# A gated delta-rule scan: diagonal inverses for two directions at once, one more unit of look-ahead, and some filler arithmetic on GpSimd

## The reference, cut to what matters

```python
decay = exp(where(tril_incl, g[..., :, None] - g[..., None, :], -inf))
lmat  = where(tril_strict, einsum('bnhid,bnhjd->bnhij', k_beta, k) * decay, 0)
t_inv = triangular_solve(eye + lmat, eye)          # inverse of a unit lower triangle
u, w  = t_inv @ v_beta, t_inv @ (k_beta * exp(g))
a_intra = where(tril_incl, einsum('bnhid,bnhjd->bnhij', q, k) * decay, 0)
def step(state, xs):                                # one chunk after the other
    v_new = u_i - w_i @ state
    o_i = (q_i * exp(g_i)) @ state + a_i @ v_new
    state = state * exp(g_last) + (k_i * exp(g_last - g_i)).T @ v_new
```

## Time and profile before

| | |
|---|---|
| Runs, median (range) | 2976.65 us (2975.73 to 2983.44), 3 runs |
| Profiled execution | 2969.94 us, its span 2968.2 us |
| Mean granted PE clock | 0.945 of full speed |
| Busy, share of the span | PE 91%, VectorE 47%, ScalarE 35%, GpSimd 20% |
| The scan | 553 to 1257 us |

### The profile page before, as it was taken

How to read it: one execution, slowest core, us unless ns; L and a number is a source line. 1 busy time by engine, 2 the same in 40 slices (tenths; PEclk the granted TensorE clock), 3 DMA queues, 4 the chain that set the end, 5 groups by cost and what they waited for, 6 DMA issues and landing times. The chain is left out here.

```text
span 2968.2 us, 46123 instructions
## 1 busy us (share of the span) xinstructions
PE 2691.4 (91%) x18134; PEld 2530.2 (85%) x18134; DVE 1406.6 (47%) x2321; ACT 1040.6 (35%) x1801; POOL 601.8 (20%) x488
## 2 busy tenths in 40 slices
PE   7999999899899999728999868989999999999999
PEld 3898999788788888726777758889999999999999
DVE  4564332156667676447888833352222242222222
ACT  4212333234234343136778733332222222222211
POOL 1001222334333433133223221210111000111100
PEclk9999999989779899858999989999999999999999
DMA  5324664343343332140000044332222233222232
GB/s 202 144 80 131 220 220 158 125 117 95 90 138 86 97 101 72 58 164 14 9 17 16 12 180 167 116 98 71 78 76 72 78 114 94 71 78 71 69 96 70
DMA packets 195643, 294.22 MB, mean 99 GB/s; under 512 B 82800, under 2 KB 121744, under 8 KB 193936
## 3 DMA queue, kind: packets, MB, share of 16 engines
q1 hardware_dynamic: 192592, 276.15, 29.9%
q10 hardware_dynamic: 2880, 15.73, 1.5%
HBM read 228.28 MB, written 63.52 MB: 98 GB/s over the span
## 5 line engine op out<-in xcount | busy, mean ns | idle before, releaser
L277 PE MATMUL f_ps<-mf_h_hi,mf_w_hi 128*128 128x320 f32 x1408 | 435.1, 309 | 1.4 <-PEq L1985 1.4
L277 PE MATMUL f_ps<-mf_h_hi,mf_w_lo 128*128 128x320 f32 x1408 | 435.1, 309 | 0.0
L277 PE MATMUL f_ps<-mf_h_lo,mf_w_hi 128*128 128x320 f32 x1408 | 435.1, 309 | 0.0
L2418 DVE TENSOR_TENSOR mf_w_lo<-mf_w_raw,mf_w_hi 128x1024 fp32r<-128x1024 f32 (+1 forms) x135 | 188.9, 1399 | 431.7 <-ACT mf_w_hi L2270 431.4
L277 PE MATMUL proj_ps<-h_hi,w_hi 128*128 128x320 f32 x896 | 282.9, 316 | 6.0 <-DVE w_lo L571 5.6
L277 PE MATMUL proj_ps<-h_lo,w_hi 128*128 128x320 f32 x896 | 278.2, 311 | 0.0
L277 PE MATMUL proj_ps<-h_hi,w_lo 128*128 128x320 f32 x896 | 278.1, 310 | 0.0
L277 PEld LDWEIGHTS f_ps<-mf_h_hi,mf_w_hi 128*128 128x128 f32 x1408 | 264.4, 188 | 1.6 <-issue 1.6
L277 PEld LDWEIGHTS f_ps<-mf_h_lo,mf_w_hi 128*128 128x128 f32 x1408 | 264.4, 188 | 0.0
L277 PEld LDWEIGHTS f_ps<-mf_h_hi,mf_w_lo 128*128 128x128 f32 x1408 | 264.4, 188 | 0.0
L2344 POOL TENSOR_TENSOR f_ff_lo<-f_ff_f,f_ff_hi 128x640 f32 (+1 forms) x44 | 69.3, 1575 | 783.4 <-ACT f_ff_hi L2270 783.4
(11 more groups left out here) (321 smaller groups left out, 6434.2 us busy)
## 6 DMA issues: line engine op xcount, KB each, us to landing
mf_w_raw<-w_up_dram SPq DMA_DIRECT2D x88, 512.0 KB, 3.5
w_raw<-w_in_dram SPq DMA_DIRECT2D x48, 512.0 KB, 4.3
w_ada_raw<-w_ada_dram SPq DMA_DIRECT2D x16, 1024.0 KB, 5.0
mf_w_raw<-w_mix_dram SPq DMA_DIRECT2D x32, 512.0 KB, 4.8
mf_w_raw<-w_down_dram SPq DMA_DIRECT2D x32, 448.0 KB, 3.3
delta_t<-delta_tile ACTq DMA_DIRECT2D x10, 1024.0 KB, 6.7
decay_t<-g_rows SPq DMA_DIRECT2D x40, 256.0 KB, 4.5
kq_t<-delta_t SPq DMA_DIRECT2D x20, 512.0 KB, 4.5
```

What stands on the lines that cost most here:

```text
L277: ins = nc.tensor.matmul(out, w(k), a(k), start=(first and n == 0 and q == 0), stop=(last and n == len(ks) - 1 and q == 2))
L2418: nc.vector.tensor_tensor(wlo[:, slot, 0:nk], raw[:, slot, 0:nk], whi[:, slot, 0:nk].bitcast(F32), ALU.subtract).then_inc(E[half]["lo"], 1)
```

## The change

- `diagonal` works for the pair of units 2j (forward) and 2j + 1 (backward) at once, on 128 partitions, in `body(u)` of odd u = 2j - 1: rows 1 to 5 in level 4, 6 to 8 in level 5, 9 in level 6, always behind the products. ScalarE turns the backward half's blocks first (`turn_backward`, at the head of odd units) and writes the pair after level 6. SP stores it with four DMAs, later in the odd unit than before (behind slot 8), and loads `x_base` with eight DMAs a unit, each of twice the pieces.
- Products are made three units ahead (`AHEAD`), decay matrices four; the scan opens at unit -4. The products stand behind the first half of levels 5 and 6.
- `kq_t` has two buffers and serves the products alone; the recurrence reads a second copy, `kq_again`, loaded once more. `n_t` and `attn_t` have five buffers. `o_stage` and `fill_stage` have one each.
- `quota` is 6 in all of the units -4 to -1: the same 312 filler matmuls. Filler groups take `bank_F` and an idle bank of `banks_bc` in turn for the first 13 groups.
- From filler tile 8 on the low part is made by GpSimd (`fill` on GpSimd).

```diff
-        H4, NU = 4, 2 * NT
+        H4, NU, AHEAD, RING = 4, 2 * NT, 3, 5
...
-        K_AT = {(LV[1], 1): 0, (LV[2], 1): 1}
+        K_AT = {(LV[1], 0): 0, (LV[2], 0): 1}
-        UNITS = range(-3, NU + 1)
+        UNITS = range(-AHEAD - 1, NU + 1)
...
-        BASE_ROWS = ((1, 2, 3, 4, 5), (6, 7), (8,), (9,))
+        BASE_AT = {LV[0]: (1, 2, 3, 4, 5), LV[1]: (6, 7, 8), LV[2]: (9,)}
...
-                return 12 if u == -1 else 6
+                return 6
...
+        OPENING = 13
+        fill_bank = lambda t, g: (BC[1][:, 1] if 2 * t + g < OPENING and g else FB)[:, 0:GN]
+        BY_POOL = 8
@@ sync @@
+            def blocks_in(j):
+                if j:
+                    sp.wait_ge(e["base_step"], BASE * j)
+                sp.wait_ge(e["blocks_out"], 256 * (j + 1))
+                for d, to in ((0, dg), (1, db)):
+                    sp.dma_start(to[64 * d:64 * d + 64], io["diag"][d].rearrange("b h j i -> (b h) (j i)")).then_inc(e["blocks_in"], 16)
+
+            def inverse_out(j):
+                sp.wait_ge(e["xo_ready"], 2 * j + 2)
+                if j:
+                    sp.wait_ge(e["xb_in"], 128 * 2 * j)
+                for d in range(2):
+                    for x in range(2):
+                        dst = io["diag_inv"][d, :, x ^ d].rearrange("b h i j -> b h (i j)")
+                        sp.dma_start(dst, xo[64 * d:64 * d + 64, x].bitcast(F32)).then_inc(e["pair_out"], 16)
...
-                    for x in range(2):
-                        sp.dma_start(XB[rows, x, :, rows].bitcast(F32), io["diag_inv"][b, :, x].rearrange("h i j -> i h j")).then_inc(e["xb_in"], 16)
+                    sp.dma_start(XB[rows].rearrange("p x h i -> p (x h) i")[:, :, rows].bitcast(F32), io["diag_inv"][k % 2, b].rearrange("x h i j -> i (x h) j")).then_inc(e["xb_in"], 16)
...
-                if has(u + 1):
-                    inverse_out(u + 1)
-                    if u == -1:
-                        sp.wait_ge(e["xb_zero"], 1)
+                if has(u + 1) and u % 2 == 0:
                     inverse_in(u + 1)
...
                 for s in range(6, 9):
                     fill(u, s)
-                if has(u + 3) and u >= 0:
+                if has(u + 1) and u % 2:
+                    inverse_out((u + 1) // 2)
+                    if u == -1:
+                        sp.wait_ge(e["xb_zero"], 1)
+                    inverse_in(u + 1)
+                if has(u + 1) and u >= 0:
                     if has(u - 1):
                         sp.wait_ge(e["qs_ps"], u)
-                    load_kq(u + 3)
-                if has(u + 2):
-                    blocks_out(u + 2)
+                    load_again(u + 1)
+                if has(u + AHEAD):
+                    blocks_out(u + AHEAD)
+                if has(u + AHEAD + 2) and u + AHEAD >= 0:
+                    load_kq(u + AHEAD + 2)
...
-                if has(u + 2):
-                    blocks_in(u + 2)
+                if has(u + AHEAD) and (u + AHEAD) % 2:
+                    blocks_in((u + AHEAD) // 2)
@@ gpsimd @@
+            def fill(u, slots):
+                for s in slots:
+                    for t in started(u, s):
+                        if BY_POOL <= t + 1 < NF:
+                            pool.wait_ge(e["fill_hi"], t + 1)
+                            nc.gpsimd.tensor_tensor(flo[:, (t + 1) % 2], fraw[:, (t + 1) % 2], fhi[:, (t + 1) % 2].bitcast(F32), ALU.subtract).then_inc(e["fill_lo_pool"], 1)
@@ scalar: body @@
+                if has(u + 1) and u % 2:
+                    turn_backward((u + 1) // 2)
...
-                    if has(u + 1) and lv == LV[1]:
-                        inverse_pair(u + 1)
+                    if has(u + 1) and u % 2 and lv == LV[2]:
+                        inverse_pair((u + 1) // 2)
@@ vector: body @@
-                    if has(u + 1) and i < 2:
-                        diagonal(u + 1, BASE_ROWS[2 * i])
-                        diagonal(u + 1, BASE_ROWS[2 * i + 1])
-                    fill(u, 3 * i)
-                    for c in range(2):
-                        if has(u + 2) and (lv, c) in K_AT:
-                            products(u + 2, K_AT[lv, c])
-                        fill(u, 3 * i + 1 + c)
+                    if has(u + AHEAD) and (lv, 0) in K_AT:
+                        products(u + AHEAD, K_AT[lv, 0])
+                    if has(u + 1) and u % 2:
+                        diagonal((u + 1) // 2, BASE_AT[lv])
+                    for s in range(3 * i, 3 * i + 3):
+                        fill(u, s)
@@ tensor: fill @@
-                    if lo == 0 and 2 * t + g:
-                        pe.wait_ge(e["fill_out"], 2 * t + g)
+                    n = 2 * t + g
+                    if lo == 0 and n > 1:
+                        pe.wait_ge(e["fill_out"], n if n >= OPENING else n - 1)
```

More of the change, by code:

```diff
@@ L775, in delta_scan @@
         vn, kd, t1 = (sb(n, [P, NH, HD]) for n in ("v_new", "k_decayed", "scan_tmp"))
-        ost = sb("o_stage", [P, 2, 512])
+        ost = sb("o_stage", [P, 512])
         fraw, fhi, flo = keep["w_raw"], keep["w_hi"], keep["w_lo"]
-        fout = sb("fill_stage", [P, 2, 2, GN])
+        fout = sb("fill_stage", [P, 2, GN])
         A = [ctx.enter_context(nc.psum_tensor(f"bank_A{e}", [P, 512], F32)) for e in range(2)]
@@ L822, in delta_scan @@
                         z_index[u, lv, c] = len(z_index)
-                    if has(u + 2) and (lv, c) in K_AT:
+                    if has(u + AHEAD) and (lv, c) in K_AT:
                         for odd in range(2):
-                            a_index["k", u + 2, K_AT[lv, c], odd] = len(a_index)
+                            a_index["k", u + AHEAD, K_AT[lv, c], odd] = len(a_index)
             for c in range(2):
@@ L938, in _ @@
             for u in UNITS:
-                if has(u + 3) and u >= -1:
-                    load_rows(u + 3)
+                if has(u + AHEAD + 1) and u + AHEAD + 1 >= 2:
+                    load_rows(u + AHEAD + 1)
                 reload(u, 0)
@@ L945, in _ @@
                     load_kv(0)
+                    load_again(0)
                 if has(u + 1) and u >= 0:
@@ L976, in _ @@
                     fill(u, s)
-                if has(u + 2):
-                    blocks_in(u + 2)
+                if has(u + AHEAD) and (u + AHEAD) % 2:
+                    blocks_in((u + AHEAD) // 2)
                 reload(u, 3)
             sp.wait_ge(e["kept"], 64)
-            for i in range(2):
-                sp.wait_ge(o_stored[i], 16 * NT)
-                sp.wait_ge(f_stored[i], 16 * (NF // 2))
+            sp.wait_ge(o_stored, 16 * NU)
+            sp.wait_ge(f_stored, 16 * NF)
         @block.gpsimd
@@ L1011, in body @@
                     decayed(u - 1)
+                fill(u, range(0, 5))
                 if has(u + 1):
@@ L1017, in body @@
                             pool.wait_ge(e["a_ps"], a_index["y", u - 1, LV[-1], c] + 1)
-                        nc.gpsimd.tensor_tensor(NI[:, k % 2, c], NTf[:, k % 4, c], idn(keep["ident"][:]), ALU.add).then_inc(e["ni_ready"], 1)
-                if has(u + 3):
-                    k = u + 3
+                        nc.gpsimd.tensor_tensor(NI[:, k % 2, c], NTf[:, k % RING, c], idn(keep["ident"][:]), ALU.add).then_inc(e["ni_ready"], 1)
+                fill(u, range(5, 9))
+                if has(u + AHEAD + 1):
+                    k = u + AHEAD + 1
                     for c in range(2):
@@ L1077, in body @@
                         fill(u, 3 * i + 1 + c)
-                    if has(u + 1) and lv == LV[1]:
-                        inverse_pair(u + 1)
-                    if has(u + 3) and lv in (LV[1], LV[2]):
-                        decay(u + 3, lv - LV[1])
+                    if has(u + 1) and u % 2 and lv == LV[2]:
+                        inverse_pair((u + 1) // 2)
+                    if has(u + AHEAD + 1) and lv in (LV[1], LV[2]):
+                        decay(u + AHEAD + 1, lv - LV[1])
                 for s in range(3 * len(LV), SLOTS):
@@ L1133, in products, with diagonal @@
                     nc.vector.tensor_tensor(n[:, odd:H4:2], ps[:, :, 1], n[:, odd:H4:2], ALU.mult)
-                    nc.vector.tensor_tensor(AT[:, k % 4, c, odd:H4:2], ps[:, :, 0], d[:, odd:H4:2], ALU.mult).then_inc(e["a_out"], 1)
+                    nc.vector.tensor_tensor(AT[:, k % RING, c, odd:H4:2], ps[:, :, 0], d[:, odd:H4:2], ALU.mult).then_inc(e["a_out"], 1)
             def view(a, offset, *dims):
                 return bass.AP(tensor=a.tensor, offset=a.offset + offset, ap=[list(a.ap[0])] + [list(d) for d in dims])
-            def diagonal(k, rows):
+            def diagonal(j, rows):
                 d, x = dg[:], xc[:]
-                si, sj = (1, 16) if k % 2 == 0 else (16, 1)
-                at = [BASE * k + STEP_AT[rows[0]]]
+                si, sj = 1, 16
+                at = [BASE * j + STEP_AT[rows[0]]]
                 def step(ins):
@@ L1245, in recur @@
                     for m in range(4):
```

(10 more changed lines are left out.)

129 lines of the change are left out of this document (70 added, 59 removed).

## The result

The changed kernel took 3002.28 us (median of 4 runs, 2996.32 to 3003.30), beside 2976.72 us for the kernel before in the same session: ratio 1.0080, 95% interval 1.0062 to 1.0099. That is 25 us slower, where 16 us faster was forecast. Its profiled execution has a span of 3000.9 us, against 2968.2. All but 1.6 us of that lies in `delta_scan`, whose first matmul starts at 554.88 instead of 553.28.

What follows compares the result with a forecast made beforehand. The prediction took the in-order matmul engine, with small holes, to bound `delta_scan`; +3.3 - 0.8 - 2.0 - 6.5 - 6.9 - 3.5 = -16.4 us gave 2960 us, range 2938 to 2982.

Steps and rivals of the forecast that it cites:

- What bounds the kernel, and the waits that go: Scan: TensorE is the bound; its `attn_t` wait falls from 27 to under 8 us, VectorE's for `diag_blocks` goes.
- Even unit 27.15 us, with the cold clock 29.35: Even scan units: 28.65 us less a 1.5 us wait gives 27.15, plus 2.2 for the lower clock after a border.
- The inverse's way back: End of odd units: products, row 9, copies, stores and loads take 30.9 us, stopping TensorE 3.0 us at nine borders.
- row 9 can't be before the products: Odd units: the argument against the rival of no border hole, which gave 2913 us at chance 0.08.
- The step that failed: Head of odd units: ScalarE waits for blocks landing 1.4 us in, needed at 3.3; margin 1.3 us, cost 0.
- Units 5 and 6: Scan units without filler, blocks late by up to 6.7 us: 71.5 us falls to 65, a gain of 6.5.
- Units 3 and 4: Scan, fourth and fifth units: 65.3 us falls to 63.3, a gain of 2.0.
- Units 0 to 2: Start of the scan: 91.8 us falls to 91.0, with unit 0 staying at 30.7 including its cold start.
- Opening +3.3: Before unit 0: the blocks wait for unit 1's products, so the opening ends 3.3 us later.
- Products one place earlier: Scan units: products ahead of the other half's matmuls get 1.4 us more lead, and a 1.5 us wait goes.
- Low parts on GpSimd: 0: Filler weights: twelve subtractions moved to GpSimd lie off the path, cost 0, bound 11 us.
- Clock: 2.2 behind each hole and no other fall: After each odd-to-even border hole the lower clock costs 2.2 us, with no other fall in the pair of units.

Runs made afterwards that it cites:

- c_way_back: The changed kernel with row 9 of the inverse in level 5, copies after level 5, inverse store and loads ahead of slot 6: 2960.88 us.
- m_heads_only: Changed kernel, way back untouched; state stores late, products early in even and late in odd units, even-unit block stores before slot 6, block reads before reload: 2965.08 us.
- l_products_back: The changed kernel with the products made where the kernel before has them, at the second halves and on VectorE behind the rows: 2986.78 us, ratio 1.0041.
- d_quota: The changed kernel with filler quotas 0, 6, 6, 12 in the opening units instead of 6 throughout: 3000.42 us, ratio 1.0077.
- n_both_quota: The changed kernel with the way back and the heads of odd units both repaired, and opening quotas 0, 6, 6, 12: 2937.97 us, ratio 0.9868.
- g_before_products: The kernel before with only the products moved, behind the first half of a level and on VectorE ahead of the diagonal chain: 3017.28 us, ratio 1.0144.
- j_odd_late: The changed kernel with earlier way back, late state stores, blocks first in the queue, and products late in odd units: 2952.64 us, ratio 0.9925.
- a_no_pool: The changed kernel with all low parts of the filler weights left to VectorE: 3000.42 us, ratio 1.0087.
- h_before_pool: The kernel before with only GpSimd making the low parts of the filler weights from the eighth tile on: 2980.41 us, ratio 1.0014.

## Why the prediction was wrong, step by step

Forecast and windows are 47.4 us apart over the scan (-16.4 and +31.0): 6.4 in the opening, 8.1 in units 0 to 2, -5.3 in units 3 and 4, 14.5 in units 5 and 6, 25.0 in units 7 to 16, -1.3 behind them.

- *What bounds the kernel, and the waits that go.* Right. `attn_t` 27.3 to 1.6 us, `y_res` 20.0 to 3.8.
- *Even unit 27.15 us, with the cold clock 29.35.* Right: 28.7 to 29.2 behind a border hole in units 8 to 16, 26.6 where the hole is repaired.
- *The inverse's way back.* Mechanism right, size near. Copies done 22.7 us in (forecast 22.0), first load 26.9 (25.7), last issue some 30.3 (29.0), TensorE 32.2 (30.9), the 1.9 us from the last issue to TensorE as forecast. The hole was 3.2 to 4.7 us instead of 3.0: the copies ended 0.7 us later, and the stores took 4.2 from first issue to first load (forecast 3.7). c_way_back removes all nine holes. What was not seen is that most of this cost can be avoided: "row 9 can't be before the products" was true of the change as written only. On VectorE row 9 fits into level 5, at the price of a wait for `y_res` of up to 2.4 us in odd units.
- *The step that failed*: "they land 1.4 us in, needed at 3.3 ... margin 1.3 us", with cost 0. Units 9, 15 and 17 do have their blocks 1.3 to 1.4 us in. But in unit 5 they land 14.2 us in, in unit 7 7.1, in unit 11 6.5, in unit 13 3.4. The margin was worked out for a unit whose queue holds nothing else. SP's program has the state's wait and stores (unit 4), reloads (units 5 and 6) and slot 8's filler store (unit 10, issued at 997.67, 0.9 us ahead of the block stores) ahead of the two reads. Two more things ate the margin. In unit 6, without filler, the products end 5.3 us ahead of the next head, not 7.9. And the second read took 2.3 to 5.6 us to land: unit 13 differs from unit 9 mostly in that (5.6 against 3.8). In units 7 to 16 the odd units hold all of the error: 181.9 us against 5 x 30.9 = 154.5, 27.4 more, 23.5 of them in units 7 and 11; even ones took 144.3 against 146.75. Of unit 7's 14.5 the stop that came last is the reload's, which the forecast has nowhere. The cost of the late heads is shown by m_heads_only against l_products_back, 20 us where the sum had 0.
- *Units 5 and 6*: forecast 65, measured 79.5, the same step at its largest, in the one place where the text itself had noted late blocks. Units 3 and 4: -2.0 forecast, -7.3 measured, unit 4 being 7 us shorter than forecast for a reason not looked into: luck, not insight.
- *Units 0 to 2*: -0.8 forecast, +7.3 measured; the granted clock fell from 0.89 to 0.78. Unit 0 began cold after the opening's 9.35 us hole and took 33.5 us, TensorE busy throughout, at 0.55. The forecast took the cold start as already in unit 0's 30.7. Unit 1 took 37.2: behind a stop of 1.76 us (at 676.2) the granted clock was 0.50 for 9.8 us, and unit 2's border hole was 4.2 us.
- *Opening +3.3*: from the scan's first matmul to unit 0 it was 10.1 us longer. The second read of blocks went out at 604.7, where 599 was forecast, its landing and the way back took 1 us more each, and VectorE 0.6. In d_quota and n_both_quota unit 0 began 6.2 and 2.3 us sooner and the time did not change clear of noise, so what the opening costs stays open.
- *Products one place earlier* was counted as pure gain. l_products_back puts it at a loss of 12 us inside the change (intervals just meeting), and g_before_products at 42 us on the kernel before. The gain for `attn_t` is real (16.8 us of waits come back in l); the rows of the inverse that now stand behind a wait for TensorE cost more. The forecast had row 9 behind the products in its border of 30.9, but did not ask what the border would be with the products left where they were.
- *Low parts on GpSimd: 0.* Right within what two runs can tell, about 9 us. One product was held up under a subtraction, see below.
- *Clock: 2.2 behind each hole and no other fall.* The first half is right: in the 4.4 us behind the nine border holes the granted clock was 0.50 or 0.51 seven times, and 0.61 and 0.69. The second is not: the falls behind the stops at the heads of units 5, 7 and 11 were 28.5, 17.2 and 12 us long.

What stays open: what unit 7 takes once the reload goes ahead of the blocks, which no run tried (it is 34 to 47 us in every version, and longest where its stop is); why the kernel with the blocks first is no faster than the one without; and where j_odd_late's gain sits.

## What to carry to other kernels

When work is batched over two steps, the chain from its last input to its first user is not halved, it moves: all of it now hangs on one place, and must be added up against each unit that has something else in the same queue, not against a quiet one. Ask of an in-order DMA queue which waits stand ahead of a transfer in program order, in every unit that is special, and which other transfers now stand behind it. And before moving an operation earlier on an engine, ask what it waits for and what then queues behind that wait: the same four VectorE operations helped `attn_t` and cost 42 us.

## What the runs showed of the hardware

Whether a short stop of TensorE brings the lower clock level was not to be read from its length alone. In the kernel with the products undone, the windows behind stops of 1.44 and of 2.44 us:

```profile
964.50:968.90 4.40, 4.40 (x38) 4.40 (x39) 2.67 (x4) 1.47 (x2) 2.95 (x3) 1.00 0.59 137
...
1149.50:1153.90 4.40, 4.40 (x20) 4.40 (x21) 1.93 (x3) 0.00 (x0) 3.79 (x4) 0.50 0.43 121
```

The first kept 1.00, yet a stop of 1.11 us in the same kernel (1029.04) was followed by 0.61, and one of 1.04 us in the kernel before with the products moved was followed by 10.7 us at 0.52. Between repeats of one kernel the time goes with the clock: the kernel before ran from 2963.63 us at a mean clock of 0.947 to 2990.22 us at 0.937.

VectorE's operations on 128 partitions took about as long as on 64: row 9's product has a median of 1.14 us in the changed kernel, 1.11 in the kernel before. Of the 60 short products (median 0.25 us) nine took 0.78 to 2.09 us, each while a GpSimd operation ran, and each ended within about 0.1 us after one. The longest was under a subtraction, the other eight under other operations of GpSimd that the kernel before has too, most often `n_t_eye`:

```profile
877.65 2.41 POOL L1042 TENSOR_TENSOR w_lo<-w_raw,w_hi 128x1024 fp32r<-128x1024 f32 x1 [3.23 <-ACT w_hi L1079]
878.08 2.09 DVE L1204 TENSOR_TENSOR diag_products<-diag_blocks,diag_inverse 128x50 f32<-128x50 f32 x1
```

The Trainium skill's GPSIMD Engine Reference (8. Key points) says that GpSimd shares its SBUF interfaces with VectorE, with contention for VectorE instructions with two SBUF inputs. These products have two, and by the nine rows the trace agrees. The time of the whole does not show where the twelve subtractions run (a_no_pool, h_before_pool).
